# A transformer trunk's two FFN entries: products A11 and A12 of the second weight tile moved ahead, around the last turns of the input

## What is computed

```
h = h + rms_norm(m, mix_post_g[i])
f = swiglu(rms_norm(h, ffn_pre_g[i]), w_ff_gate[i], w_ff_up[i], w_ff_down[i])
h = h + rms_norm(f, ffn_post_g[i])

def swiglu(x, w_gate, w_up, w_down):
    return (jax.nn.silu(x @ w_gate) * (x @ w_up)) @ w_down
```

## Time and profile before

| | us |
|---|---|
| median of three executions | 1969.14 (1968.25 to 1970.37) |
| the profiled execution, its own time | 1969.14 |
| its span in the trace | 1966.9 |
| around the span | 2.24 |
| TensorE busy | 1918.4, 98% of the span |
| VectorE busy | 1411.5, 72% |
| ScalarE busy | 897.0, 46% |

### The profile page before, as it was taken

The page is one execution under the profiler, slowest core; times in us unless marked ns, Lnnn a source line. Parts: engine busy times, 40 slices in busy tenths (PEclk is TensorE's granted clock), DMA queues, the critical chain, the costliest instruction groups (busy, mean ns, idle before and its releaser), DMA issues.

```text
span 1966.9 us, 28696 instructions
## 1 busy us (share of the span) xinstructions
PE 1918.4 (98%) x9198; PEld 1575.5 (80%) x9198; DVE 1411.5 (72%) x2384; ACT 897.0 (46%) x1726; POOL 459.2 (23%) x448
## 2 busy tenths in 40 slices
PE   7799999999999999999999999999999999999998
PEld 7778888888888878888866787788888888888787
DVE  6987777777777786575389658777777777777863
ACT  5644344444444454341178545444444444444531
POOL 3311222212222221010046211212122221222310
PEclk9999999999999999999999999999999999999999
DMA  5333322233333350254200113233332223335201
GB/s 211 107 97 97 96 88 88 75 106 91 100 92 92 89 201 27 78 219 172 86 12 1 65 43 120 74 104 94 97 95 90 87 75 105 91 107 179 95 29 68
DMA packets 221159, 189.02 MB, mean 96 GB/s; under 512 B 11168, under 2 KB 198944, under 8 KB 221088
## 3 DMA queue, kind: packets, MB, share of 16 engines
q1 hardware_dynamic: 217712, 183.38, 29.1%
q10 hardware_dynamic: 3376, 4.73, 0.7%
HBM read 167.10 MB, written 20.97 MB: 96 GB/s over the span
## 4 chain that ended last, share of the span: by engine, by line
PE 89%; DVE 6%; issue 2%; ACT 1%; DMA 1%; POOL 1%; DVEq 0%; ACTq 0%; POOLq 0%
PE ps L825 14%; PE ps L827 14%; PE ps L826 14%; PE ps L315 7%; PE ps L317 7%; PE ps L316 7%; PE ps L924 7%; PE ps L922 7%; PE ps L923 7%; PE ps L1633 2%; PE ps L1714 1%; PE ps L1687 1%; PE ps L388 1%; PE ps L631 1%; DVE w_ple_gate_lo L291 1%
## 5 line engine op out<-in xcount | busy, mean ns | idle before, releaser
L1247 DVE TENSOR_TENSOR H<-H,ps 128x512 f32<-128x512 f32 x496 | 328.0, 686 | 112.8 <-PE ps L924 111.9
L1109 POOL TENSOR_TENSOR s_raw<-s_raw,a_raw 128x512 f32<-128x512 f32 x66 | 87.4, 1326 | 766.4 <-DVE s_lo L1160 650.5
L825 PE MATMUL ps<-t_hi,s_hi 128*128 128x512 f32 x528 | 206.3, 391 | 6.9 <-DVE t_lo L1259 4.0
L826 PE MATMUL ps<-t_lo,s_hi 128*128 128x512 f32 x528 | 205.5, 389 | 0.0
L827 PE MATMUL ps<-t_hi,s_lo 128*128 128x512 f32 x528 | 205.4, 389 | 0.0
L998 ACT ACTIVATE m<-ps 128x512 f32<-128x512 f32 x44 | 26.4, 600 | 264.3 <-PE ps L827 261.9
L825 PE MATMUL ps<-b_hi,a_hi 128*128 128x512 f32 x352 | 137.0, 389 | 0.0
L826 PE MATMUL ps<-b_lo,a_hi 128*128 128x512 f32 x352 | 137.0, 389 | 0.0
L827 PE MATMUL ps<-b_hi,a_lo 128*128 128x512 f32 x352 | 136.9, 389 | 0.0
L922 PE MATMUL ps<-wd_hi,d_ab_hi 128*128 128x512 f32 x336 | 130.7, 389 | 0.0
L923 PE MATMUL ps<-wd_lo,d_ab_hi 128*128 128x512 f32 x336 | 130.7, 389 | 0.0
(11 more groups left out here) (293 smaller groups left out, 5029.8 us busy)
## 6 DMA issues: line engine op xcount, KB each, us to landing
a_raw<-in_w_ff_gate SPq DMA_DIRECT2D x88, 256.0 KB, 2.9
a_raw<-in_w_ff_up SPq DMA_DIRECT2D x88, 256.0 KB, 3.0
s_raw<-in_w_ff_up SPq DMA_DIRECT2D x88, 256.0 KB, 2.9
s_raw<-in_w_ff_gate SPq DMA_DIRECT2D x88, 256.0 KB, 3.0
wd_raw<-in_w_ff_down SPq DMA_DIRECT2D x44, 512.0 KB, 4.3
residual_spill<-H SPq DMA_DIRECT2D x16, 512.0 KB, 2.6
raw<-in_w_ple_gate SPq DMA_DIRECT2D x16, 512.0 KB, 5.5
back<-residual_spill SPq DMA_DIRECT2D x16, 512.0 KB, 5.2
```

Source lines behind the costliest of these rows:

```text
L825: pe.matmul(ps[:, bank, :], w[0], x[0], start=fresh and k == 0, stop=False, skip_group_check=not fresh)
L826: pe.matmul(ps[:, bank, :], w[0], x[1], start=False, stop=False, skip_group_check=not fresh)
L1109: eng.tensor_tensor(form_raw(name), W_RAW[name][:, :, :], form_raw(other) if other != "A21" else W_RAW["A21"][:, :, :], op).then_inc(summe ...
L1247: dve.tensor_tensor(dst, dst, src, ALU.add).then_inc(F["summed"], 1)
```

## The change

- TensorE: in both layers A11(1) now stands ahead of the last turn (of row tile 7), and A12(1) right behind it, where the 12 small matmuls of `keep_busy` stood. In layer 0, A12(0) moves ahead of the turn of row tile 6. Tile 1 is left with S2, S3, S1, A22, S4 in this order.
- Banks: A11(1) and A12(1) are summed in bank 3, the others of tile 1 in 5, 6, 7, so that they are independent of tile 0's. 
- Weight forms: A11(1) and A12(1) have raw, hi and lo places of their own (those of the down products' inputs, `d_ac` and `d_ab`, which are still unused then), and S1(1) a raw place `s1_ahead`; their loads are issued ahead.
- VectorE: A11(1)'s lo part is made ahead of the last turn's forms: in layer 0 behind `fn_normed` of row tile 7, in layer 1 ahead of `add_post` of row tile 7. A12(1)'s follows `fn_normed`. In tile 1 the four `wd_sums` are behind A22's lo part.
- ScalarE: `copy_first` of tile 1 follows `fn_raw` of row tile 7; A22(1)'s hi part follows `copy_m7` of tile 1; the four `wd_his` come together; the second silu half of tile 1 stands at its end.

```diff
-ORDER_FIRST = ("A11", "A12", "S3", "S2", "S1", "A22", "S4")
+ENTRY = (("A11", 0), ("A12", 0), ("A11", 1), ("A12", 1), ("S3", 0), ("S2", 0), ("S1", 0), ("A22", 0), ("S4", 0),
+         ("S2", 1), ("S3", 1), ("S1", 1), ("A22", 1), ("S4", 1))
...
+        ahead_hi = {"A11": as_form(Z["d_ac_hi"][:, :, :]), "A12": as_form(Z["d_ab_lo"][:, 0:2, :])}
+        ahead_lo = {"A11": as_form(Z["d_ac_lo"][:, :, :]), "A12": as_form(Z["d_ab_lo"][:, 2:4, :])}
+        ahead_raw = {"A11": as_form(Z["d_ac_raw"][:, :, :]), "A12": as_form(Z["d_ab_raw"][:, 2:4, :]),
+                     "S1": as_form(Z["s1_ahead"][:, 0:2, :])}
...
+        def bank_for(b, g, t):
+
+            if is_first(g, t):
+                return 4 if b == 3 else b
+            if is_second(g, t):
+                return 3 if b == 0 else b + 4
+            return b
...
+        def ffn_pe_ahead(pe, name, L):
+
+            if name == "A12":
+                pe.wait_ge(F["copied"], nth_copy(0, L, 0, 1))
+            ffn_product(pe, name, L, 0, 1)
...
             ffn_product(pe, "A11", L, g, t)
-            fn_turn(pe, L, PAIRS - 1, 0)
+            if L == 1:
+                fn_turn(pe, L, PAIRS - 1, 0)
             pe.wait_ge(s["added"][0], s.done("added", PAIRS - 1))
+            pe.wait_ge(*ready("A12", L, g, t))
             ffn_pe_prime(pe, "A12", 2)
             pe.wait_ge(F["copied"], nth_copy(0, L, g, t))
             ffn_product(pe, "A12", L, g, t)
+            if L == 0:
+                fn_turn(pe, L, PAIRS - 1, 0)
+            ffn_pe_ahead(pe, "A11", L)
+            pe.wait_ge(s["added"][1], s.done("added", PAIRS - 1))
+            ffn_pe_prime(pe, "A12", 4, 5)
             fn_turn(pe, L, PAIRS - 1, 1)
-            keep_busy(pe, 12, 3)
+            ffn_pe_ahead(pe, "A12", L)
             pe.wait_ge(F["t"], 4 * L + 1)
             ffn_product(pe, "S3", L, g, t)
...
+        def ffn_pe_second(pe, L):
+
+            g, t = 0, 1
+            pe.wait_ge(*ready("S2", L, g, t))
+            ffn_pe_prime(pe, "S2", 6)
+            for name in ("S2", "S3"):
+                ffn_product(pe, name, L, g, t)
+            pe.wait_ge(F["copied"], nth_copy(2, L, g, t))
+            for name in ("S1", "A22"):
+                ffn_product(pe, name, L, g, t)
+            pe.wait_ge(F["up1"], 1 + tau(L, g, t) + 1)
             ffn_product(pe, "S4", L, g, t)
...
             copy_first(act, L, g, t)
             if L == 0:
                 first_hi(act, L)
+                for name in ("A11", "A12"):
+                    form_hi(act, name, L, 0, 1)
+            else:
+                form_hi(act, "A11", L, 0, 1)
             fn_raw(act, L, PAIRS - 1, 0)
             fn_squares(act, L, PAIRS - 1, 1)
+            if L == 1:
+                form_hi(act, "A12", L, 0, 1)
...
             fn_raw(act, L, PAIRS - 1, 1)
+            copy_first(act, L, 0, 1)
...
+            if is_second(g, t):
+                copy_u(act, L, g, t)
+                copy_m7(act, L, g, t)
+                form_hi(act, "A22", L, g, t)
+                form_hi(act, "S4", L, g, t)
+                wd_his(act, L, g, range(4))
...
             fn_normed(dve, L, PAIRS - 1, 1)
             if L == 0:
+                form_lo(dve, "A11", L, 0, 1)
+            form_lo(dve, "A12", L, 0, 1)
+            if L == 0:
                 form_lo(dve, "S3", L, g, t)
...
-            form_lo(dve, "A11", L, *n)
             form_sum(dve, "S3", L, *n)
             up_second_half(dve, L, g, t)
...
+            if is_second(g, t):
+                times_up(dve, L, *p, 1)
+                form_sum(dve, "S4", L, g, t)
+                form_lo(dve, "A22", L, g, t)
+                wd_sums(dve, L, g)
+                form_lo(dve, "S4", L, g, t)
+                up_second_half(dve, L, g, t)
+                wd_los(dve, L, g, (0, 1))
+                up_first_half(dve, L, g, t)
+                times_up(dve, L, g, t, 0)
+                form_lo(dve, "A11", L, *n)
+                form_sum(dve, "S3", L, *n)
+                wd_los(dve, L, g, (2, 3))
+                form_sum(dve, "S1", L, *n)
+                form_sum(dve, "S2", L, *n)
+                form_lo(dve, "S3", L, *n)
+                d_sums(dve, L, g, 0)
+                return
...
                 sp.wait_ge(s["used"][0], s.done("used", PAIRS - 1))
                 ffn_load(sp, "S3", "a11", L, *first)
                 ffn_load(sp, "S1", "a22", L, *first)
+                sp.wait_ge(s["used"][1], s.done("used", PAIRS - 1))
+                ffn_load(sp, "A11", "a11", L, 0, 1)
+                ffn_load(sp, "A12", "a12", L, 0, 1)
...
                 if L == 1:
                     for name in ("S3", "S2", "S1"):
                         form_lo(dve, name, L, 0, 0)
+                    form_lo(dve, "A11", L, 0, 1)
                 add_post(dve, s_before, PAIRS - 1, 1)
```

More of the change, by code:

```diff
@@ L749, in ready @@
             vector, pool = 1 + L * 7 * (GROUPS + 1), 1 + L * 7 * (GROUPS - 1)
-            if is_first(g, t):
-                return F["form"]["vector"], vector + ORDER_FIRST.index(name) + 1
+            if isinstance(g, int) and g == 0:
+                return F["form"]["vector"], vector + ENTRY_LO[L].index((name, t)) + 1
             if t == 1:
-                if name in early and not (isinstance(g, int) and g == 0):
+                if name in early:
                     return F["form"]["pool"], pool + 7 * g - 3 + early.index(name) + 1
@@ L806, in ffn_load_tile @@
                 n = following(g, t)
-                ffn_load_after(sp, "A11", "a11", L, *n, (g, t))
+                if not is_first(g, t):
+                    ffn_load_after(sp, "A11", "a11", L, *n, (g, t))
                 sp.wait_ge(*summed("S4", L, g, t))
@@ L810, in ffn_load_tile @@
                 for name, source in (("S3", "a11"), ("S2", "a22"), ("A12", "a12"), ("S1", "a22")):
-                    ffn_load_after(sp, name, source, L, *n, (g, t))
+                    if not (is_first(g, t) and name in ("A12", "S1")):
+                        ffn_load_after(sp, name, source, L, *n, (g, t))
             if t == 0 and not is_first(g, t):
@@ L818, in ffn_product @@
         def ffn_product(pe, name, L, g, t):
-            bank = {"A11": 0, "A12": 0, "S2": 1, "S1": 1, "S4": 1, "A22": 2, "S3": 3}[name]
+            bank = bank_for({"A11": 0, "A12": 0, "S2": 1, "S1": 1, "S4": 1, "A22": 2, "S3": 3}[name], g, t)
+            forms_ = weight_form(name, g, t)
             fresh = name in ("A11", "S3")
@@ L1048, in ffn_act_first @@
             n = following(g, t)
-            for name in ("A11", "S3", "S2", "A12", "S1"):
+            for name in ("S3", "S2", "S1"):
                 form_hi(act, name, L, *n)
         def ffn_act_tile(act, L, g):
-            t, p, n, down = 0, preceding(g, 0), following(g, 0), g - 1
-            gate_silu(act, L, *p, 1)
+            t, n, down = 0, following(g, 0), g - 1
             form_hi(act, "S2", L, g, t)
@@ L1095, in ffn_act_second @@
                 form_hi(act, "S3", L, *n)
+                gate_silu(act, L, g, t, 1)
         def form_sum(eng, name, L, g, t):
@@ L1108, in form_sum @@
                 eng.wait_ge(*summed("S1" if name == "S2" else other, L, g, t))
-            eng.tensor_tensor(form_raw(name), W_RAW[name][:, :, :], form_raw(other) if other != "A21" else
+            own = ahead_raw[name] if is_second(g, t) and name in ahead_raw else W_RAW[name][:, :, :]
+            eng.tensor_tensor(form_raw(name, g, t), own, form_raw(other, g, t) if other != "A21" else
                                W_RAW["A21"][:, :, :], op).then_inc(summed(name, L, g, t)[0], 1)
@@ L1293, in ffn_dve_first @@
             times_up(dve, L, g, t, 0)
-            for name in ("A12", "S1"):
-                form_lo(dve, name, L, *n)
+            form_lo(dve, "S1", L, *n)
         def ffn_dve_tile(dve, L, g, first_group=False):
```

85 lines of the change are left out of this document (56 added, 29 removed), and 3 rows, old and new, of the table ENTRY_LO.

## The result

| | before | after |
|---|---|---|
| median | 1970.85 (17 executions, 1968.25 to 1972.03) | 1974.08 (17, 1971.57 to 1975.18) |
| ratio | | 1.0017, 95% interval 1.0010 to 1.0023 |
| span of the profiled execution | 1966.9 | 1970.9 |
| mean granted TensorE clock over the executions | 0.9973 (three later sets: 76 executions) | 0.9954 |

3.2 us lost, 0.17%: slower, since the interval leaves out 1, and by about 0.2% at most (its upper end is 0.23%). The prediction was 1971.0 (1966.5 to 1974.3), on a median of 1969.14 for the kernel before; with more executions that median is 1970.85. So 1.7 us of the 3.1 between prediction and result belong to the kernel before, 1.3 to the change (3.2 lost for 1.9).

The account below looks back on a forecast made before the run. TensorE, busy 1918.4 of 1966.9 us, was taken as the bound, with VectorE setting the time at the entry. 1.0 - 1.1 + 1.7 + 0.3 = 1.9 lost on 1969.1 gave 1971.0 us, range 1966.5 to 1974.3.

Parts of the forecast that it names:

- The likeliest case: Layer 0's turn held behind A11(1), VectorE's tails, the clock low once: 1971.0 us (1969.5 to 1972.8); chance 0.50.
- slower: Clock low into a second stretch in layer 0, and falling in layer 1 too: 1973.2 to 1975 us; chance 0.18.
- steps 1 to 5: Layer 0 up to S3(1): last turn waits behind A11(1), 4.1 us later; S3(1) starts at 116.95.
- step 6: Layer 0, S3(1) to down products: VectorE's chain takes 20.55 us; 0.8 us lost, 1.0 with added hops.
- Layer 1: Layer 1's entry up to the down products: they start at 1249.75 in place of 1250.87, 1.1 us gained.
- the fourth: Layer 1, S3(0) to S1(0): of 7.46 us about 0.7 of waits (for t2) goes; S1(0) at 1217.95.
- The clock: TensorE's clock falls after layer 0's wait of about 5.7 us: 1.7 us lost; layer 1: 0.3 as a mean.
- faster: Both layers: the moved products pay, second tile at PE's pace: 1964 us, or 1967.5 if half; chance 0.12.

Follow-up runs that it names:

- e10: Changed kernel plus 20 small useless matmuls ahead of A11(1) in layer 0, five and seven around the last turn in layer 1: 1970.89 us, 1.0001 of before.
- e1: Changed kernel with A11(1)'s lo part behind `add_post` of row tile 7 in layer 0 alone: 1968.87 us, 0.9992 of the kernel before.
- e9: e5 with GpSimd's sum for S4(0) held back until t1's lo part is made, in layer 1 alone: 1961.59 us, 0.9953 of the kernel before.
- e8: Changed kernel with GpSimd's sum for S4(0) held back until t1's lo part is made, in layer 1 alone: 1973.06 us, 1.0014 of before.
- e2b: Changed kernel plus 5 small useless matmuls ahead of the last turn and 7 behind it, in layer 1: 1973.67 us, 1.0015 of the kernel before.
- e5: Changed kernel with A11(1)'s lo part behind `add_post` in both layers and the second tile's sums and copies in their old order: 1962.04 us, 0.9961 of before.
- e6: Kernel before without the 12 small matmuls behind the last turn in both layers: 1971.51 us, 1.0007 of the kernel before.
- e3: Changed kernel with A11(1)'s lo part behind `add_post` of row tile 7 in both layers: 1967.43 us, 0.9987 of the kernel before.
- e2: Changed kernel plus 20 small useless matmuls ahead of A11(1) in layer 0: 1971.28 us, 1.0007 of the kernel before.
- e4: Changed kernel with the second tile's sums and copies for the down weights in their old order: 1967.56 us, 0.9984 of the kernel before.
- e11: e9 with GpSimd's sum for S4(0) held back in layer 0 as well: 1964.39 us, 0.9967 of the kernel before.
- e7: e5 plus five small useless matmuls ahead of the last turn and seven behind it in layer 1: 1963.57 us, 0.9966 of the kernel before.

## Why the prediction was right, and where it was off

**Verdict.** A small loss within 0.2%, as forecast at 0.70: 3.2 us for 1.9. The likeliest case was the right one in kind: the turn of layer 0 held behind A11(1), VectorE's tail, the clock low. That 1974.08 stands only 0.2 under the upper end of the range, and above the 1973.1 that was taken for 0.2% slower, is owed as much to the starting value as to the change: the median of three executions was 1.7 lower than that of 17. Half of the rival "slower" came true as well: the clock fell in layer 1 too, at the 1.2 us that it had named. Its other half did not: in layer 0 the clock was back at 1.00 from 94, ahead of A12(1). The prediction also took 0.2% for the least that can be told from no change; 17 executions of each told 0.17%.

**Layer 0's order, steps 1 to 5: right.** Turn 83.02 (83.2 forecast), A11(1) at 89.67 (89.9), the last turn at 93.17 with the clock kept up (e10; 93.2) and 94.91 without (95). L577, the L567 of before, waited 3.81. e1 shows that the cause is the lo part's place: moved, the wait ahead of A11(1) is 1.75 for 5.62 and the last turn comes 5.4 us sooner behind the one before it.

**The tail, step 6: right in kind, a little large.** Waits ahead of S4(1), A11(2), S3(2): 0.43, 1.25, 1.51 for 0.6, 1.3, 1.6; 3.16 of idle VectorE ahead of A22(1)'s lo part for 3. Down products of layer 0 with the clock at 1.00: 137.27, that is 0.55 lost for the 1.0 forecast.

**Layer 1: mis-sized, 1.1 gained forecast, 0.2 found** (53.52 in e10 for 53.72). `add_post` came 2.1 later relative to the turn ahead, as forecast (2.2). The step that failed is the fourth, "about 0.7 of that (for t2) goes, as PE is now later than DVE". PE in layer 1 of e1_lo_l0, whose edit leaves layer 1 as in the kernel after and whose clock was at 1.00 there: S3(0), S2(0) and S1(0).

```profile
1212.65 0.50 PE L868 MATMUL ps<-t_hi,s_hi 128*128 128x512 f32 x1 [0.37 <-DVE t_lo L1348]
...
1216.38 0.50 PE L868 MATMUL ps<-t_hi,s_hi 128*128 128x512 f32 x1 [0.70 <-DVE t_lo L1348]
...
1220.11 0.47 PE L868 MATMUL ps<-t_hi,s_hi 128*128 128x512 f32 x1 [0.72 <-issue]
```

The waits ahead of S3(0) and S2(0) are there, since A12(1)'s lo part took 1.77 us, and from the last turn (1206.51) to S1(0) it took 13.60 for the 12.45 forecast. In e9, where that lo part took 0.69 and the clock was at 1.00, it took 12.28 (from the turn at 1202.43):

```profile
1214.71 0.47 PE L868 MATMUL ps<-t_hi,s_hi 128*128 128x512 f32 x1 [0.72 <-issue]
```

With the lo part undisturbed, the step comes out as it was forecast. The prediction costed the lo part with the distance of undisturbed rows, 0.60, in a stretch where GpSimd's sum was sure to run: a lo part of that size in the trace of the kernel before, beside that same sum, would have told, 1.19 for 0.69. DVE and POOL there:

```profile
1207.56 1.19 DVE L1259 TENSOR_TENSOR t_lo<-t_raw,t_hi 128x512 fp32r<-128x512 f32 x1
```

```profile
1206.93 1.28 POOL L1109 TENSOR_TENSOR s_raw<-s_raw,a_raw 128x512 f32<-128x512 f32 x1 [5.24 <-DMA s_raw<-in_w_ff_gate]
```

e8 shows the sum to be what stretches it.

**The clock: mis-sized, 2.0 forecast, 3.1 in the profiles and 3.2 in the medians** (the kernel after against e10). Layer 0: 1.7 forecast, 1.9 found from turn to down (55.97 for 54.07), and 2.5 and 2.4 in the profiles of e2b and e8, whose clock fell there too. Layer 1: 0.3 taken as a mean, 1.18 found in the profiled execution (54.70 for 53.52), the cap being 1.2. The mistake was to weigh one trace's fall in layer 1 as something that the change could not make worse. The mean clock over the executions went from 0.9973 to 0.9954, 3.7 us of full-speed work.

**The rest.** 0.3 between the entries and 0.4 behind the last, which the prediction costed at nothing, are of the size by which the profiles differ there anyway (over all runs 1060.4 to 1061.3 from down products to the next turn, and 715.9 to 716.5 behind layer 1's), and no cause is claimed. So two errors of the order's terms partly cancelled (0.5 too much lost in layer 0, 0.9 too much gained in layer 1), and the clock's term was 1.1 too small. The rival "faster" was not wrong about the stake: with the lo parts and the tail in place (e5), 8.5 us of the 10.9 are there.

## What to carry to other kernels

A product moved into a hole is moved with its whole supply: its hi and lo parts want to be early on their engines, or what stands behind it in TensorE's order waits for them too, and 5.6 us of one new wait outweigh two holes of 2.7. Look for what the hole was good for: here small matmuls kept the clock up, worth about 1 us while TensorE waits for VectorE (e6, and the interval includes nothing), worth 3 us as soon as products stand there (e10). And when an instruction is put beside another engine's, cost it by a row that had that neighbour.

## What the runs showed of the hardware

- VectorE and GpSimd hold each other up. A VectorE instruction with two SBUF inputs that started beside a GpSimd sum took 0.5 to 1.1 us more: 1.19 for 0.69, 1.77 for 0.68, 2.21 and 2.32 for 1.28, 3.37 for 2.28. It goes the other way too: GpSimd's sum took 3.22 us in layer 0, beside a lo part of 2.28, 2.02 in layer 1 of the kernel after, begun beside `tmp`, and 1.29 by itself. The Trainium skill (SBUF — State Buffer, "SBUF: two separate sides") says that such a pair locks a shared port for the whole instruction and the later one blocks; by that rule the late one loses what is left of the other. The rows agree to 0.2 us: A12(1)'s lo part began at 1207.86, the sum ended at 1209.09, and 1.23 + 0.68 is 1.91 for 1.77 measured.
- The clock's fall is not a matter of one wait's length. 5.62 us in layer 0 had the clock at 0.50 in the profiles of all four kernels that had it; the wait of 1.67 ahead of A12(1) in layer 1 had it in the kernel after, e3, e5 and e8, and not in e1, e2, e4, e9 or e11; the same wait in layer 0 had it in e9 and not in e1, e3, e5, e7 or e11. Also, five of the profiles (e1, e4, e5, e7, e9) show 3.4 us lost between 60 and 72 us, ahead of the first entry, in code that the change does not touch, and the profile of the kernel before does not. One profile is a sample; the mean clock over all executions is the better witness.
